# Wide moving operands, an adding transfer and a dropped row scale in the Strassen stage of a two layer trunk

## The reference, cut to what matters

```python
def rms_norm(x, gain):
    y = xf * lax.rsqrt(jnp.mean(xf * xf, axis=-1, keepdims=True) + EPS)
    return (y * gain).astype(x.dtype)
def conv_mixer(h, w_in, conv_w, w_out):
    u, b_gate, c_gate, z = jnp.split(h @ w_in, 4, axis=-1)     # 512 x 2048 @ 2048 x 8192
    y = b_gate * causal_depthwise_conv(c_gate * u, conv_w)
    return (y * jax.nn.silu(z)) @ w_out
...
    x = x + rms_norm(conv_mixer(rms_norm(x, norm_pre[1]), ...), norm_post[1])
```

## Time and profile before

| | |
|---|---|
| median of 3 runs | 2366.77 us |
| the profiled execution | 2368.34 us |
| its span | 2366.5 us |
| PE busy | 2315.4 us (98%) |
| DVE busy | 1574.9 us (67%) |
| ACT busy | 943.7 us (40%) |
| POOL busy | 226.9 us (10%) |

### The profile page before, as it was taken

How to read it: one execution, slowest core, us unless ns; L and a number is a source line. 1 busy time by engine, 2 the same in 40 slices (tenths; PEclk the granted TensorE clock), 3 DMA queues, 4 the chain that set the end, 5 groups by cost and what they waited for, 6 DMA issues and landing times.

```text
span 2366.5 us, 34093 instructions
## 1 busy us (share of the span) xinstructions
PE 2315.4 (98%) x13689; PEld 2005.3 (85%) x13689; DVE 1574.9 (67%) x2063; ACT 943.7 (40%) x1581; POOL 226.9 (10%) x157
## 2 busy tenths in 40 slices
PE   8999999999999999999999899999999999999998
PEld 6788888888787888888787778999999999788776
DVE  6676767664456557733475789888888888433855
ACT  5233333333344446522244444444444444322444
POOL 4000000001010101011130410000000000010400
PEclk9999999999999999999999899999999999999999
DMA  5322222232322224632221233233333224424122
GB/s 202 99 76 81 75 80 84 71 94 89 112 85 72 91 79 160 205 110 86 80 89 65 80 133 112 108 112 116 108 116 108 107 108 157 146 80 134 63 72 89
DMA packets 84874, 244.57 MB, mean 103 GB/s; under 512 B 16992, under 2 KB 20224, under 8 KB 84736
## 3 DMA queue, kind: packets, MB, share of 16 engines
q1 hardware_dynamic: 84256, 241.06, 30.1%
q10 hardware_dynamic: 480, 1.59, 0.2%
HBM read 231.59 MB, written 11.03 MB: 103 GB/s over the span
## 4 chain that ended last, share of the span: by engine, by line
PE 89%; DVE 7%; issue 2%; ACT 2%; DMA 0%; POOL 0%; DVEq 0%; ACTq 0%; SPq 0%
PE acc L1130 17%; PE acc L1132 16%; PE acc L1131 16%; PE m L1629 4%; PE m L1632 4%; PE m L1631 4%; PE acc L1629 3%; PE acc L1632 3%; PE acc L1631 3%; PE acc L1488 2%; PE acc L1489 2%; PE acc L1493 2%; DVE weights_lo L1659 1%; PE m L1304 1%; PE m L1312 1%
## 5 line engine op out<-in xcount | busy, mean ns | idle before, releaser
L1130 PE MATMUL acc<-input_hi,weights_hi 128*128 128x512 f32 (+1 forms) x1880 | 745.4, 396 | 21.2 <-DVE weights_lo L1659 20.6
L1132 PE MATMUL acc<-input_hi,weights_lo 128*128 128x512 f32 (+1 forms) x1880 | 721.8, 384 | 0.0
L1131 PE MATMUL acc<-input_lo,weights_hi 128*128 128x512 f32 (+1 forms) x1880 | 721.0, 384 | 0.0
L1659 DVE TENSOR_TENSOR weights_lo<-weights_raw,weights_hi 128x1024 fp32r<-128x1024 f32 x288 | 396.2, 1387 | 184.0 <-ACT weights_hi L599 183.3
L1130 PEld LDWEIGHTS acc<-input_hi,weights_hi 128*128 128x128 f32 x1880 | 355.2, 189 | 102.2 <-DVE weights_lo L1659 22.5
L1132 PEld LDWEIGHTS acc<-input_hi,weights_lo 128*128 128x128 f32 x1880 | 354.6, 189 | 71.7
L1131 PEld LDWEIGHTS acc<-input_lo,weights_hi 128*128 128x128 f32 x1880 | 355.6, 189 | 64.8 <-issue 1.9
L599 ACT ACTIVATE weights_hi<-weights_raw 128x1024 fp32r<-128x1024 f32 x288 | 298.9, 1057 | 182.4 <-PE acc L1132 153.7
L1629 PE MATMUL m<-input_hi,weights_hi 128*128 128x256 f32 x672 | 191.5, 285 | 5.5 <-DVE weights_lo L2347 2.7
L1632 PE MATMUL m<-input_hi,weights_lo 128*128 128x256 f32 x672 | 190.9, 284 | 0.0
L1631 PE MATMUL m<-input_lo,weights_hi 128*128 128x256 f32 x672 | 190.8, 284 | 0.0
(11 more groups left out here) (377 smaller groups left out, 4145.5 us busy)
## 6 DMA issues: line engine op xcount, KB each, us to landing
weights_raw<-in_ab_w_in SPq DMA_DIRECT2D x126, 512.0 KB, 3.7
weights_raw<-in_c_w_in SPq DMA_DIRECT2D x72, 512.0 KB, 4.8
work<-in_c_w_in SPq DMA_DIRECT2D x42, 512.0 KB, 3.8
weights_raw<-in_m_w_kv SPq DMA_DIRECT2D x32, 512.0 KB, 3.8
weights_raw<-in_ab_w_out SPq DMA_DIRECT2D x32, 512.0 KB, 4.1
weights_raw<-in_m_w_q SPq DMA_DIRECT2D x32, 512.0 KB, 3.6
weights_raw<-in_c_w_out SPq DMA_DIRECT2D x32, 512.0 KB, 4.5
residual<-in_x SPq DMA_DIRECT2D x32, 256.0 KB, 5.6
```

Of the source, the lines that this page charges most:

```text
L1130: pe.matmul(out, w_hi[:, o:o + P], hi(kt), start=kt == first_kt, stop=False)
L1131: pe.matmul(out, w_hi[:, o:o + P], lo(kt), start=False, stop=False)
L1132: last = pe.matmul(out, w_lo[:, o:o + P], hi(kt), start=False, stop=kt == last_kt)
L1659: TTO(w_lo[:, s * CW:(s + 1) * CW], raw[:, c * CW:(c + 1) * CW], w_hi[:, s * CW:(s + 1) * CW].bitcast(F32), ALU.subtract).then_inc(lo_read ...
```

## The change

1. A product of the stage has two matmuls a tile where it had three: the high weights times high and low input in one matmul of 512 columns, 256 of each, into the two halves of a PSUM bank, and the low weights times the high input in one of 256 into the first half. The high and low input now lie in one tensor (H_both), 8192 elements apart.
2. The two halves of a bank are added as they are evacuated: 12 DVE instructions a pair where there were 5. The order of the products is A11, S3, S1, A12, S2, S4, A22.
3. S3 is no longer a DVE sum. SP loads one quarter of the weights into S3's place, and POOL issues a transfer that adds the other quarter to it.
4. b is not multiplied by rs any more, nor its plain pair; y is too small or large by a factor of its token. The norm behind scales its EPS for that (`eps_rows`).
5. The first tap of the convolution is two ACT instructions.
6. The sums of the input are made in blocks of four tiles, 1024 elements an instruction, and the first block earlier; two splits of c_w_out are done between parts of `last_input`.

```diff
-S_ORDER = ("A11", "S3", "A12", "S1", "S2", "S4", "A22")
-S_BANK, S_FRESH = (0, 1, 0, 2, 1, 2, 1), (0, 1, 3, 5)
+S_ORDER = ("A11", "S3", "S1", "A12", "S2", "S4", "A22")
+S_BANK, S_FRESH = (0, 1, 2, 0, 1, 2, 1), (0, 1, 2, 5)
-TURNED_AT = {10: (0,), 11: (1, 2), 12: (3,), 13: (4, 5), 14: (6,), 15: (7,)}
+SUMS_AT, HIGHS_AT, LOWS_AT = {9: 0, 13: 1}, {10: 0, 13: 1}, {11: 0, 14: 1}
...  wino_product (PE)
-                elif pos == 2:
-                    pe.wait_ge(s_p1, q + 1)
...
-                    pe.wait_ge(s_ev, evacs(q, "v5" if pos == 5 else "C22"))
+                    pe.wait_ge(s_ev, evacs(q, {3: "p1", 5: "v5", 6: "C22"}[pos]))
-                    pe.matmul(out, w_hi[:, o:o + P], moving(pos, kt, 0), start=kt == 0 and pos in S_FRESH, stop=False,
-                              skip_group_check=True)
-                    pe.matmul(out, w_hi[:, o:o + P], moving(pos, kt, 1), start=False, stop=False, skip_group_check=True)
-                    last = pe.matmul(out, w_lo[:, o:o + P], moving(pos, kt, 0), start=False, stop=kt == 7,
+                    both, high = moving(pos, kt)
+                    pe.matmul(out.rearrange("p (a n) -> p a n", a=2), w_hi[:, o:o + P], both,
+                              start=kt == 0 and pos in S_FRESH, stop=False, skip_group_check=True)
+                    last = pe.matmul(high_half(out), w_lo[:, o:o + P], high, start=False, stop=kt == 7,
...  s_loads (SP)
+                if q > 1:
+                    sp.wait_ge(s_lo, 7 * (q - 1) + 2)
+                    s_load(q, 2, s_s3(q), s3_in)
...  POOL, behind norm 1
+            def wino_sums(q):
+                block = 4 * (8 * (0, 2, 1, 3)[q % 4] + q // 4 + 1)
+                quarter = lambda at_: dram["c_w_in"][P * (block + at_):P * (block + at_ + 1), :]
+                pool.wait_ge(s3_in, 16 * (q + 1))
+                pool.dma_start(s_s3(q), quarter(0), accum_op=ALU.add).then_inc(s_sum["S3"], 16)
...  weight_sum (DVE)
-                if name == "S3":
-                    dve.wait_ge(s_in["r0", q % 2], 16 * (q // 2 + 1))
-                    dve.wait_ge(s_in["r2", q % 2], 16 * (q // 2 + 1))
-                    if q == 1:
-                        dve.wait_ge(chunk_used, C_C + 16)
-                    TTO(s_s3(q), r2, r0, ALU.add).then_inc(s_sum["S3"], 1)
...  evacuate_product (DVE)
+                if pos == 0:
+                    TTO(p1, low, p1, ALU.add).then_inc(s_ev, 1)
+                elif pos == 2:
+                    TTO(v5, high, p1, ALU.add).then_inc(s_ev, 1)
+                    TTO(v5, low, v5, ALU.add).then_inc(s_ev, 1)
+                elif pos == 3:
+                    TTO(c00, low, c00, ALU.add).then_inc(s_ev, 1)
                 elif pos == 4:
+                    TTO(v5, high, v5, ALU.add).then_inc(s_ev, 1)
+                    STT(out=c11, in0=low, scalar=-1.0, in1=v5, op0=ALU.mult, op1=ALU.subtract).then_inc(s_ev, 1)
-                    TTO(base, corner_of(j, 1, 1), v7, ALU.add).then_inc(s_ev, 1)
+                    TTO(base, c11, high_half(v7), ALU.add).then_inc(s_ev, 1)
+                    TTO(base, base, low_half(v7), ALU.add).then_inc(s_ev, 1)
...  conv_step (DVE)
-                elif step == 16:
-                    for k in range(2):
-                        TS(cv[:, o], cu[:, o], pcol("c_conv", (2 * n + k) * 3 + 2), None, ALU.mult).then_inc(*WV.did())
-                    TTO(head2(bb), head2(bb), both_rows(rs[:, :]), ALU.mult).then_inc(*WV.did("br"))
...  wino_group (ACT)
+                    if s == 16:
+                        act.wait_ge(*WV("scaled", r))
+                        for k in range(2):
+                            act.activation(cv[:, o], cu[:, o], ACT.Copy, scale=pcol("c_conv", (2 * n + k) * 3 + 2))\
...  behind the last product (DVE)
             last_input(0, 4)
             evacuate_product(S_PAIRS - 1, 6)
-            last_input(4, 8)
             WV.round(7)
             finish(7, 0)
+            last_input(4, 8)
+            split(C_OUT1 + 2)
             finish(7, 4)
             finish(7, 5)
-            last_input(8, 16)
+            last_input(8, 12)
+            split(C_OUT1 + 3)
+            last_input(12, 16)
```

More of the change, by code:

```diff
@@ L330, in build, with moving @@
         s_source = lambda q, name: s_s3(q) if name == "S3" else s_raw[home[name]][q % 2]
[L332 to L346, removed]
+        four = lambda t, k, h: t.rearrange("p (k n) -> p k n", n=T)[:, k:k + 4, h * HT:(h + 1) * HT]
+        fourths = lambda b: Y[:, 10 * T + 4 * b * HT:10 * T + 4 * (b + 1) * HT].rearrange("p (k n) -> p k n", n=HT)
+        before_first, before_second, before_third = (lambda b, k=k, t=t: four(t, 4 * b + k, 1) for k, t in ((0, X), (8, X), (0, Y)))
+        def moving(pos, kt):
+            if pos in (1, 2, 4):
+                tile_, k = ((turned_y, kt), (turned_x, kt), (turned_x, kt + 8))[(1, 2, 4).index(pos)]
+                both = tile_[:, k * T:(k + 1) * T].rearrange("p (a n) -> p a n", a=2)
+            else:
+                k, h = ((kt, 0), (kt + 8, 0), (kt + 8, 1), (kt, 1))[(0, 3, 5, 6).index(pos)]
+                both = H_both.rearrange("p (a k n) -> p a k n", a=2, n=T)[:, :, k, h * HT:(h + 1) * HT]
+            return both, both[:, 0, :]
         s_bank = lambda q, pos: ((m01[:, 0, :], m01[:, 1, :], m23[:, 0, :]),
-                                 (m23[:, 1, :], acc[2], acc[3]))[q % 2][S_BANK[pos]][:, 0:HT]
+                                 (m23[:, 1, :], acc[2], acc[3]))[q % 2][S_BANK[pos]][:, 0:T]
+        high_half, low_half = (lambda t: t[:, 0:HT]), (lambda t: t[:, HT:T])
         bank = lambda pair, n, width=T: acc[2 * (pair % 2) + n][:, 0:width]
@@ L1607, in wino_product @@
                 pe.wait_ge(s_lo, i + 1)
-                if pos in (0, 1, 3):
+                if pos in (0, 1, 2):
                     if q == 0:
@@ L2170, in sum_squares @@
                     TS(stat[:, 0:4], M[0][:, 0:4], 1.0 / D, EPS, ALU.mult, ALU.add).then_inc(*NV.did("stat2"))
+                    if r == 1:
+                        dve.wait_ge(*NV.last())
+                        TS(eps_rows, stat[:, 0:4], EPS, None, ALU.mult).then_inc(*SV.did("eps_rows"))
             def next_rows(r):
@@ L2448, in evacuate_product @@
+                    dve.wait_ge(s_ev, evacs(q, "C12a"))
+                    TTO(c01, low, c01, ALU.add).then_inc(s_ev, 1)
                 elif pos == 6:
-                    STT(out=corner_of(j, 1, 0), in0=out, scalar=-1.0, in1=p1, op0=ALU.mult, op1=ALU.subtract)\
-                        .then_inc(s_ev, 1)
+                    TTO(p1, high, p1, ALU.add).then_inc(s_ev, 1)
+                    dve.wait_ge(s_ev, evacs(q, "C21a"))
+                    STT(out=c10, in0=low, scalar=-1.0, in1=p1, op0=ALU.mult, op1=ALU.subtract).then_inc(s_ev, 1)
@@ L2621, in _ @@
                 power(stat, powed, 4).then_inc(*NG.did("pow2"))
+                if r == 1:
+                    for q in range(S_PAIRS):
+                        wino_sums(q)
             for t in range(TT):
```

187 lines of the change are left out of this document (96 added, 91 removed).

## The result

| | before | after |
|---|---|---|
| median | 2366.60 us (2366.32 to 2368.14, 4 runs) | 2339.54 us (2338.99 to 2340.39, 4 runs) |
| ratio of medians | | 0.9885, 95% interval 0.9868 to 0.9902 |
| the profiled execution | 2368.34 | 2339.35 |
| its span | 2366.5 | 2337.5 |
| stage, first matmul to the first behind it | 569.7 | 557.5 |

The forecast was 2338 us. Between the two profiled executions lie 29.0 us. I paired the matmuls outside the stage, whose number is the same, by their count, and read off where the lead grows: 1.6 us ahead of everything that was changed (the profiled execution of before is itself 1.7 over its median), 10.4 between the norm and the stage, 12.2 in the stage, 5.9 behind it, and 1.0 lost in a norm further on.

A forecast was written before the change was run, and what follows sets the result against it. PE, 98% busy, was taken to set the pace with DVE near behind. Gains of 12.7 in the stage, 10.0 ahead and 5.9 behind made 28.6 us: 2368.3 to 2339.7 profiled, median 2338; range 2328 to 2355 for 8 in 10.

The forecast's parts named there:

- PE's own work: Stage matmuls: a tile takes 0.347 us after for 0.360 now, over 1568 tiles 20.4 us less.
- the first rival: Stage matmuls: the width change pays the 0.013 us again, PE gains nothing by merging; 2349 us, 7 in 100.
- The 2.5 ns of the Trainium skill: Page's surplus per back to back matmul; by it the edit is worth 3.9 us; the forecast went by the rows.
- DVE's load: DVE in the stage: net +5.1 us a group, 75.0 of 77.7 us of matmuls; still fits.
- the tight stretch: Pos 0 of a group's third pair to C22: DVE needs 17.8 us against 16.7, PE waits 1.15.
- The two lighter places: Low halves at pos 4 of the fourth pair and pos 3 of the second come 0.2 to 0.3 us late.
- The stage: Its length, PE's work, clock and waits together: 569.2 to 556.5 us, gain 12.7.
- Ahead of it: Before the stage: cheaper input sums, first block inside DVE's row scale wait; stage starts 10.5 us sooner, 10.0 taken.
- Behind it: After the stage: third low half of c_w_out earlier, no wait or half clock; gain 5.9 us.
- The adding transfer: POOL's transfer making S3: some 12 us from issue to landing, so it costs 0; upper bound 28 us.
- The rival of a late transfer: S3's adding transfer takes 15 us, each pair waits 3: 84 us, some 2422; 6 in 100.
- DVE as the bound: Stage: waits take the upper bound of 4 us a group, 2353 us; 16 in 100.

The follow-up runs named there:

- run 6: Changed kernel with four DVE steps of a group moved and a product's eight 512 column matmuls ahead of its eight of 256: 2328.8 us, stage 548.8.
- run 1: Changed kernel with the 512 column matmul cut into two of 256 (full sums not computed): 2349.5 us, stage 568.3.
- run 3: Changed kernel with the two matmuls of every second tile exchanged: 2337.4 us, stage 555.8.
- run 4: Changed kernel with four DVE steps of a group moved to where DVE has more room: 2335.3 us, stage 553.7.
- run 7: Changed kernel with the first block of input sums late again and the old order behind the stage: 2351.0 us, stage 559.3.
- run 8: Changed kernel with the input's sums and low halves made tile by tile, 256 elements a DVE instruction: 2343.0 us, stage 558.5.
- run 10: Changed kernel with the load of S3, and with it the adding transfer, issued four products later: 2555.4 us, stage 777.2.
- run 2: Changed kernel with S3 made by DVE again, one 128x1024 instruction a pair, without its transfers: 2369.5 us, stage 586.8.
- run 11: Changed kernel with b multiplied by the row scale again, one 128x1024 DVE instruction a group: 2342.9 us, stage 561.5.
- run 12: Changed kernel with the first tap back on DVE, two 128x512 instructions a group, none on ACT: 2342.3 us, stage 561.5.

## Why the prediction was right, and where it wasn't

The time was right to 1.5 us and the three parts of the sum nearly exact (28.6 us forecast, 28.5 measured), but the part of the stage is right by luck: it came out of two errors that cancel. The 1.5 us are the step from the profiled execution to the median. For the profiled one the sum gave 2339.7, and it took 2339.35; before's lies 1.6 us over the median and has the 1.6 us ahead of everything that was changed; the changed kernel's lies 0.2 under its own.

- **PE's own work** was mis-sized: 20.4 us forecast, 12.8 measured. The step that failed is "0.227 + 0.120 after", taken from rows in which all matmuls were alike. It holds only in the fast pace. In turn the widths fall into a slow pace of 0.353, and 107 of 182 products are in it: 6.3 of the 7.6 us. The rest is the kernel before, whose products are 2.873 in the mean and not 2.880, since those of turned_third take 2.83. The bound of 0 to 0.026 a tile held it; the first rival (the surplus is paid again) was half true, though not as a price of each change, as run 6 shows. That the edit brings PE's gain is shown by run 1.
- **The 2.5 ns of the Trainium skill** (TensorE: Matmul & The Clock Gate, "Wait — 56ns, not 53.3ns?") would have given 3.9 us. Run 1 has 10.8, so its rule for the surplus doesn't hold for these matmuls, and mine of 13 ns holds in rows alike: run 6 has 0.227 and 0.120 at the end of its rows of eight.
- **DVE's load** was right: 93% of a 79.6 us group is 74.3 us for 75.0. So was the tight stretch: from pos 0 of the third pair to the release 17.8 us forecast, 17.8 measured. The wait was 0.9 where 1.2 was forecast, since six products took 16.95 us and not 16.66: PE's slow pace comes out of its wait. The two lighter places didn't show at all. So 7.2 us of waits in the stage where 13.8 were forecast. This is the 7 us by which PE's term was too large, and runs 3 and 4 show the two in exchange.
- **The stage**: 12.7 forecast, 12.2 measured; the group 79.4 and 79.6. The forecast let the stage of before end at 2008.3; the first matmul behind it starts at 2008.78, so its length is 569.7 and not 569.2.
- **Ahead of it**: 10.0 forecast, 10.4 measured, first matmul at 1427.0 for "about 1429" (1.6 of it is the profiled execution's earlier lead). DVE had its first low half ready about half a microsecond before PE came. Runs 7 and 8 show both halves of the reasoning, 4.0 and 3.8 us; what the remaining 2.6 are is open.
- **Behind it**: 5.9 forecast and measured; run 7 shows it by the order alone.
- **The adding transfer**: 0 taken, and in 27 pairs ACT never waits for it; landing in 5.4 us where 8 was the limit. My allowance of 12 us from issue to landing is 11 (in one pair POOL issued at 1552.8 and ACT wanted the sum at 1563.8). The rival of a late transfer has the right mechanism, its price was too low: run 10 loses 220 us, where 5.8 us late in each of 28 pairs would be 162.
- **The Trainium skill's rule on the shared port** (SBUF — State Buffer, "SBUF: two separate sides") didn't show. DVE's 128x1024 instructions take 1.22 us as before, and POOL's issue 0.88.
- **DVE as the bound** (the second rival) was nearer than its 16 in 100 say: 1.13 us more a pair is 30 us (run 2).

Not foreseen: the norm behind lost 1.0 us. The windows view of before and of after, 30 us there each, has the clock at 0.89 and 0.83.

```profile
2180.00:2210.00 30.00, 26.47 (x122) 22.09 (x122) 18.30 (x24) 9.37 (x14) 8.99 (x6) 0.89 0.15 48
```

```profile
2150.00:2180.00 30.00, 26.45 (x118) 22.13 (x117) 17.39 (x23) 9.37 (x14) 8.22 (x6) 0.83 0.12 39
```

It doesn't go with the change: in both kernels PE has a wait of 1.6 us from start to start there (at 2191.4 and 2161.3), behind which the clock is 1.00 in the one and 0.50 in the other. Of the twelve experiments, eleven of which have the changed norm, five lose 0.9 to 1.4 us there and seven 0.4 or less.

## What to carry to other kernels

A price per instruction that is read where all instructions are alike may be too low where two kinds alternate, as it was here for most products; look at a pattern's period in the trace and try another order, which cost nothing here and brought 7 us more once DVE's waits were gone. An engine at 93% beside one at 99% has no free place, all the less when most of its idle time is spent waiting for a third: take work from it before adding to it. Of 1 us more a group a half to two thirds came out (runs 11 and 12), of 4.5 us more a group nearly all (run 2). When two engines are near each other in the same stretch, a part of a gain on one is lost in its wait for the other, so remove both losses together (1.7 and 3.8 us apart, 10.5 together).

## What the runs showed of the hardware

- Matmuls of 512 and 256 columns in turn run at 0.347 or 0.353 us a pair, and can keep the slow pace for 172 products on end (run 4). In the changed kernel each group was in the fast one within four products of its wait, and most changes of pace fall at products of turned_third.
- The clock fell to its lower level after some waits of PE and not after others as long. Run 2 has seven of 2.65 to 3.16 us from start to start: behind four (2.66, 2.86, 2.86, 3.16) the starts of wide matmuls were 0.426 us apart for a while, behind three (2.65, 2.65, 2.86) not. In the norm behind, the same wait of 1.6 us left it at 1.00 in the kernel before and at 0.50 in the changed one.
- A transfer that adds to SBUF (512 KB) lands 5.4 us after POOL's issue as placed in the changed kernel, 9.8 in run 10, where it meets other loads.
